# A decoder layer with 32 experts: the expert weights fetched in 2 MB transfers of 16 KB rows, in ten double slots

## What is computed

```python
logits = xt @ w_router + b_router
top_val, top_idx = lax.top_k(logits, 4)
gate = softmax(top_val)
# for each expert e that has rows:
hb = x_pad[rows] @ w_up[e] + b_up[e]                 # w_up[e]  1024 x 2048
glu = minimum(hb[:, :1024], 7); lin = clip(hb[:, 1024:], -7, 7)
act = glu * sigmoid(1.702 * glu) * (lin + 1)
y = act @ w_down[e] + b_down[e]                      # w_down[e] 1024 x 1024
```

## Time and profile before

| | |
|---|---|
| median of 3 runs | 1215.26 us (1214.33 to 1217.21) |
| profiled execution, span | 1214.7 us |
| TensorE busy | 1131.6 us, 93% of the span |
| DMA, q1 (all weight transfers) | 88.9% of 16 engines' span, 441.65 MB |
| HBM read over the span | 364 GB/s |
| SyncE waiting for TensorE in L459 (L1472 and L1508) | 182.4 us |

### The profile page before, as it was taken

How to read it: one execution, slowest core, us unless ns; L and a number is a source line. 1 busy time by engine, 2 the same in 40 slices (tenths; PEclk the granted TensorE clock), 3 DMA queues, 4 the chain that set the end, 5 groups by cost and what they waited for, 6 DMA issues and landing times.

```text
span 1214.7 us, 14754 instructions
## 1 busy us (share of the span) xinstructions
PE 1131.6 (93%) x5609; PEld 506.6 (42%) x5609; DVE 359.5 (30%) x766; ACT 227.4 (19%) x415; POOL 128.5 (11%) x59
## 2 busy tenths in 40 slices
PE   6899999989999999999999979999999899999996
PEld 5788899753333333233333323323222233222222
DVE  4593664632222222122223212222222122222222
ACT  5344554121111111111111111111111111111112
POOL 5562566300000000000000000000000000000000
PEclk9999999989999999999999989999999999999999
DMA  9554235779999999999999999999999999999993
GB/s 355 188 188 147 95 139 190 302 315 359 423 421 421 421 422 419 420 421 421 421 421 421 421 420 421 421 421 421 422 421 421 420 421 422 421 421 421 421 421 145
DMA packets 77890, 444.33 MB, mean 366 GB/s; under 512 B 9166, under 2 KB 12664, under 8 KB 28664
## 3 DMA queue, kind: packets, MB, share of 16 engines
q1 hardware_dynamic: 75904, 441.65, 88.9%
q10 hardware_dynamic: 1912, 1.66, 0.5%
HBM read 441.65 MB, written 1.05 MB: 364 GB/s over the span
## 4 chain that ended last, share of the span: by engine, by line
PE 55%; DMA 19%; SPq 15%; DVE 5%; ACT 3%; issue 3%; POOL 0%; DVEq 0%; ACTq 0%
PE psum L1472 21%; SPq L459 15%; PE psum L1173 11%; PE psum L1508 11%; DMA ring<-in_w_up 9%; DMA gate_area<-in_w_up 5%; DMA qk_area<-in_w_up 4%; PE psum L1427 3%; PE psum L1360 2%; DVE gate_area L1110 1%; DVE gate_area L1106 1%; DVE gate_area L1104 1%; PE psum L1495 1%; ACT gate_area L766 1%; PE psum L1481 1%
## 5 line engine op out<-in xcount | busy, mean ns | idle before, releaser
L1472 PE MATMUL psum<-ring,gate_area 128*64 128x512 f32 x1312 | 311.4, 610 | 28.4 <-DMA ring<-in_w_up 18.4
L1076 DVE TENSOR_TENSOR h_s<-psum,h_s 128x512 f32<-128x512 f32 x132 | 82.0, 683 | 433.2 <-PE psum L1427 433.2
L1472 PEld LDWEIGHTS psum<-ring,gate_area 128*64 128x64 f32 x1312 | 90.2, 139 | 234.5 <-issue 170.6
L1508 PE MATMUL psum<-ring,gate_area 128*64 128x512 f32 x640 | 145.8, 595 | 5.3 <-ACT gate_area L766 5.3
L531 POOL TENSOR_TENSOR unit_lo<-ring,unit_hi 128x1024 fp32r<-128x1024 f32 (+1 forms) x54 | 128.1, 2377 | 95.5 <-ACT unit_hi L564 95.4
L760 ACT ACTIVATE gate_area<-gate_area 128x512 f32<-128x512 f32 x32 | 20.1, 629 | 545.5 <-DVE gate_area L1102 545.5
L1102 DVE TENSOR_SCALAR gate_area<-psum 128x512 f32<-128x512 f32 x32 | 22.1, 692 | 283.5 <-PE psum L1481 283.5
L1508 PEld LDWEIGHTS psum<-ring,gate_area 128*64 128x64 f32 x640 | 44.4, 136 | 86.2 <-issue 76.9
L1427 PE MATMUL psum<-pT_s,gate_area 64*128 64x512 f32 x264 | 65.6, 615 | 0.7 <-ACT pT_s L770 0.7
L564 ACT ACTIVATE unit_hi<-ring 128x1024 fp32r<-128x1024 f32 (+1 forms) x54 | 55.5, 1032 | 47.5 <-PE psum L1173 47.4
L1408 PE MATMUL psum<-xn_area,gate_area 128*64 128x512 f32 x264 | 63.8, 604 | 0.4 <-DVE gate_area L1048 0.4
(11 more groups left out here) (256 smaller groups left out, 1229.1 us busy)
## 6 DMA issues: line engine op xcount, KB each, us to landing
ring<-in_w_up SPq DMA_DIRECT2D x164, 1024.0 KB, 26.5
ring<-in_w_down SPq DMA_DIRECT2D x80, 1024.0 KB, 26.9
gate_area<-in_w_up SPq DMA_DIRECT2D x16, 1024.0 KB, 27.0
xT_area<-in_w_up SPq DMA_DIRECT2D x16, 1024.0 KB, 27.1
ring<-in_w_gate SPq DMA_DIRECT2D x6, 2048.0 KB, 8.7
qk_area<-in_w_up SPq DMA_DIRECT2D x12, 1024.0 KB, 26.5
mem_s<-in_w_up SPq DMA_DIRECT2D x12, 1024.0 KB, 28.2
yl_area<-in_w_up SPq DMA_DIRECT2D x12, 1024.0 KB, 26.9
```

What stands on the lines that cost most here:

```text
L1076: nc.vector.tensor_tensor(h_s[:, b, cols], psum[:, BACK_BANKS[j], :], h_s[:, b, cols], ALU.add).then_inc(added, 1)
L1472: ins = nc.tensor.matmul(psum[lo:lo + SLOTS, c, :], lhsT, w[:, at:at + 512], start=(k == 0), stop=False)
L1508: ins = nc.tensor.matmul(psum[c * SLOTS:(c + 1) * SLOTS, DOWN_BANK, :], lhsT, w[:, at:at + 512], start=(f == 0), stop=(f == KC - 1))
```

## The change

Two neighbouring pieces become one of 2 MB (`PIECE_W` is 4096 numbers, 16 KB, per partition). An expert has 4 up pieces and 2 down pieces. `w_up` is regrouped on the host so that partition p of a piece holds rows p of two chunks side by side, and `w_down` so that a piece is contiguous; every DMA is then one contiguous 2 MB block of 16 KB rows. There are ten slots: six in `ring`, four in areas that are made by putting the former areas side by side: `qe_area` (qk and 8 KB per partition that are new), `gm_area` (end of gate and mem), `xv_area` (xT and vp), `my_area` (memT and yl). `ROUND_SKIPS` leaves slot 5 out of the second round and slot 8 out of the fourth, so that a group of 48 pieces closes. TensorE computes the same chunks in the same order; it signals `piece_used` after every second chunk. GpSimd's descriptor scratch is set to 1 KB; GpSimd issues no DMA in either kernel. `graw` lies in `misc` now.

```diff
-PIECES = UP_CHUNKS + DOWN_SLOTS
-WSLOTS = 19
+PIECE_W = 2 * UP_W
+UP_PIECES = UP_CHUNKS // 2
+DOWN_PIECES = DOWN_SLOTS // 2
+PIECES = UP_PIECES + DOWN_PIECES
+WSLOTS = 10
 GROUP = 8
-SLOT_OF = [n % (WSLOTS - 1) + 1 for n in range(5 * (WSLOTS - 1))]
-for _n in (0, 19, 37, 54, 69, 83):
-    SLOT_OF.insert(_n, 0)
+ROUND_SKIPS = ((), (5,), (), (8,), ())
+SLOT_OF = [s for skips in ROUND_SKIPS for s in range(WSLOTS) if s not in skips]
...
-                if n < UP_CHUNKS:
-                    src_w, dst = w_up[0][bass.ds(e, 1), n * P:(n + 1) * P, :].rearrange("a p n -> (a p) n"), wslot[slot]
+                if n < UP_PIECES:
+                    src_w = w_up[bass.ds(e, 1), n, :, :].rearrange("a p n -> (a p) n")
                 else:
-                    j = n - UP_CHUNKS
-                    src_w = w_down[bass.ds(e, 1), :, j * DOWN_W:(j + 1) * DOWN_W].rearrange("a p n -> (a p) n")
-                    dst = wslot[slot]
-                sp.dma_start(dst, src_w).then_inc(got_piece[slot], 16)
+                    src_w = w_down[bass.ds(e, 1), n - UP_PIECES, :, :].rearrange("a p n -> (a p) n")
+                sp.dma_start(wslot[slot], src_w).then_inc(got_piece[slot], 16)
...
-                            w = piece(u, k, n_group)
+                            w = piece(u, k // 2, n_group)[:, k % 2 * UP_W:(k % 2 + 1) * UP_W]
...
-                            if k < UP_CHUNKS - 1:
+                            if k % 2 == 1 and k < UP_CHUNKS - 1:
                                 ins.then_inc(piece_used, 1)
...
-                            w = piece(u, UP_CHUNKS + j, n_group)
+                            w = piece(u, UP_PIECES + j // 2, n_group)[:, j % 2 * DOWN_W:(j % 2 + 1) * DOWN_W]
...
-                            ins.then_inc(piece_used, 1)
+                            if j % 2 == 1:
+                                ins.then_inc(piece_used, 1)
...
-    nc = bacc.Bacc("TRN2", target_bir_lowering=False, num_devices=1)
+    nc = bacc.Bacc("TRN2", target_bir_lowering=False, num_devices=1, dynamic_dma_scratch_size=1024)
...
+    up = data["w_up"].reshape(NE, UP_PIECES, 2, P, UP_W)
+    data["w_up"] = np.ascontiguousarray(up.transpose(0, 1, 3, 2, 4)).reshape(NE, UP_PIECES, P, PIECE_W)
+    down = data["w_down"].reshape(NE, DOWN_PIECES, 4, P, D)
+    data["w_down"] = np.ascontiguousarray(down.transpose(0, 1, 3, 2, 4)).reshape(NE, DOWN_PIECES, P, PIECE_W)
```

More of the change, by code:

```diff
@@ L187, in hybrid_layer_kernel, with at @@
         xn_parts = nc.alloc_sbuf_tensor_at("xn_parts", [P, 8, S], F32R, offset=xn_at)
-        mem_at = nc.sbuf_base + (-nc.sbuf_base) % 32
-        mem_s = sb("mem_s", [P, B, D])
-        mem_parts = nc.alloc_sbuf_tensor_at("mem_parts", [P, 2, S], F32R, offset=mem_at)
+        def at(name, shape, offset, dt=F32):
+            return nc.alloc_sbuf_tensor_at(name, shape, dt, offset=offset)
+        gm_at = nc.sbuf_base + (-nc.sbuf_base) % 32
+        gm_area = sb("gm_area", [P, 3 * KC * S + B * D])
+        gate_area = at("gate_area", [P, 3 * KC, S], gm_at)
+        mem_at = gm_at + 4 * 3 * KC * S
+        mem_s = at("mem_s", [P, B, D], mem_at)
+        mem_parts = at("mem_parts", [P, 2, S], mem_at, F32R)
+        qe_at = nc.sbuf_base + (-nc.sbuf_base) % 32
+        qe_area = sb("qe_area", [P, PIECE_W])
+        qk_area = at("qk_area", [P, 2 * HEADS // 2 * S], qe_at)
         xT_at = nc.sbuf_base + (-nc.sbuf_base) % 32
-        xT_area = sb("xT_area", [P, KC * S])
-        xT_hi = nc.alloc_sbuf_tensor_at("xT_hi", [P, KC, S], F32R, offset=xT_at)
+        xv_area = sb("xv_area", [P, PIECE_W])
+        xT_area = at("xT_area", [P, KC * S], xT_at)
+        xT_hi = at("xT_hi", [P, KC, S], xT_at, F32R)
+        vp_area = at("vp_area", [P, 2 * HEADS * HD + 2 * B * S], xT_at + 4 * KC * S)
         memT_at = nc.sbuf_base + (-nc.sbuf_base) % 32
[L195 to L202, removed]
+        my_area = sb("my_area", [P, KC * M + 6 * S + 2 * (P + S)])
+        memT = at("memT", [P, KC, M], memT_at)
+        memT_parts = at("memT_parts", [P, 8, S], memT_at, F32R)
+        yT_at = memT_at + 4 * KC * M
+        yl_area = at("yl_area", [P, 6 * S + 2 * (P + S)], yT_at)
+        yT_parts = at("yT_parts", [P, 4, S], yT_at, F32R)
         ib_area = sb("ib_area", [P, S + 2 * (P + S)])
@@ L214, in hybrid_layer_kernel @@
         rope_t = sb("rope_t", [P, 2, 8, ROPE])
-        graw = sb("graw", [64, P])
         gT = sb("gT", [P, 64])
@@ L274, in hybrid_layer_kernel @@
         iw_s = view(misc, 768, B, IHEADS)
+        graw = view(misc, 1024, P)[0:64]
         pooledT = view(pT_s, 0, G, S)
@@ L299, in hybrid_layer_kernel @@
         hot = view(gate_area, 3712, SLOTS // 2).bitcast(BF16)
-        wslot = [ring[:, n * UP_W:(n + 1) * UP_W] for n in range(PIECES)]
-        wslot += [xT_area[:, :], view(mem_s, 0, UP_W), view(gate_area, 4096, UP_W), view(memT, 0, UP_W)]
-        wslot += [view(area, 0, UP_W) for area in (qk_area, vp_area, yl_area)]
+        wslot = [ring[:, n * PIECE_W:(n + 1) * PIECE_W] for n in range(PIECES)]
+        wslot += [view(qe_area, 0, PIECE_W), view(gm_area, 4096, PIECE_W), view(xv_area, 0, PIECE_W),
+                  view(my_area, 0, PIECE_W)]
         y_s = view(pT_s, 0, D // 2)
@@ L451, in load @@
             def load(e, n, slot):
-                if n < UP_CHUNKS:
-                    src_w, dst = w_up[0][bass.ds(e, 1), n * P:(n + 1) * P, :].rearrange("a p n -> (a p) n"), wslot[slot]
-                else:
-                    j = n - UP_CHUNKS
-                    src_w = w_down[bass.ds(e, 1), :, j * DOWN_W:(j + 1) * DOWN_W].rearrange("a p n -> (a p) n")
-                    dst = wslot[slot]
-                sp.dma_start(dst, src_w).then_inc(got_piece[slot], 16)
+                if n < UP_PIECES:
+                    src_w = w_up[bass.ds(e, 1), n, :, :].rearrange("a p n -> (a p) n")
+                else:
+                    src_w = w_down[bass.ds(e, 1), n - UP_PIECES, :, :].rearrange("a p n -> (a p) n")
+                sp.dma_start(wslot[slot], src_w).then_inc(got_piece[slot], 16)
             last = {n % RING_SLOTS: name for n, name in enumerate(FRONT)}
             def load_over(name):
-                for q in range(UP_CHUNKS):
-                    if last[q // 2] == name:
+                for q in range(RING_SLOTS):
+                    if last[q] == name:
                         load(0, q, q)
@@ L476, in _ @@
                       .then_inc(got_parts, 16)
-            sp.wait_ge(bank_filled, FILLED["gate", 3 * KC - 1])
-            load(0, 11, 11)
             sp.wait_ge(bank_filled, FILLED["o", MHEADS + HEADS - 1])
-            load(1, 4, 16)
+            load(1, 0, 6)
             sp.wait_ge(lo_ready, LAST_SPLIT["P"])
@@ L484, in _ @@
             sp.wait_ge(bank_filled, FILLED["br", KC - 1, 2])
-            for q in range(8, 11):
+            for q in range(4, 6):
                 load(0, q, q)
             sp.wait_ge(got_parts, 24 * 16)
-            load(1, 1, 13)
             sp.wait_ge(merged_ready, KC)
-            load(1, 2, 14)
-            load(1, 6, 18)
+            load(1, 1, 7)
             for name in ("O0", "O1"):
@@ L494, in _ @@
                 load_over(name)
-            load(1, 0, 12)
             sp.wait_ge(scaled, 4 * B)
-            load(1, 5, 17)
+            load(1, 2, 8)
             sp.wait_ge(bank_filled, FILLED["logits"])
-            load(1, 3, 15)
+            load(1, 3, 9)
             def load_group(g, first):
@@ L1557 @@
     data["norm_final_g"] = data["norm_final_g"].reshape(1, D)
-    data["w_down"] = np.ascontiguousarray(data["w_down"].reshape(NE, KC, P, D).transpose(0, 2, 1, 3)).reshape(NE, P, KC * D)
+    up = data["w_up"].reshape(NE, UP_PIECES, 2, P, UP_W)
+    data["w_up"] = np.ascontiguousarray(up.transpose(0, 1, 3, 2, 4)).reshape(NE, UP_PIECES, P, PIECE_W)
+    down = data["w_down"].reshape(NE, DOWN_PIECES, 4, P, D)
+    data["w_down"] = np.ascontiguousarray(down.transpose(0, 1, 3, 2, 4)).reshape(NE, DOWN_PIECES, P, PIECE_W)
     for k, v in shape_constants().items():
```

## The result

The changed kernel takes 1203.12 us (median of 4 runs, 1202.4 to 1203.21) against 1215.26 us: 12.1 us less. The ratio is 0.9896, 95% interval 0.9883 to 0.9909. Measured once more later, beside the kernel before, it was 0.991 (0.9882 to 0.9938).

What follows compares the result with a forecast made beforehand. The DMA stream was taken as the bound: span 1214.7 - 10.4 (16 KB rows) + 1.0 (fill and first rounds) + 1.7 (end) = 1207.0, plus 0.6 to the median, said as 1207.5 us. Range 1202 to 1219, the forecast's own 1202 to 1213.

Steps and rivals of the forecast that it cites:

- What bounds: Expert stretch: the DMA stream sets the end, 956 us at 421 GB/s; TensorE is 2.7 us faster per expert.
- 16 KB rows: Weight stream: 1728 fewer packets per engine at 6 ns each, from 2, 4 and 8 KB row times, save 10.4 us.
- The stated upper bound: On the saving from 16 KB rows: 9.3 ns a packet, 16.1 us, using the last five 2 KB slices.
- rival C: Weight stream: a packet costs 9.3 ns, saving 16.1 us, time 1202; part of the forecast's own 0.70.
- Half as many transfers: Full weight stream: a fixed time per transfer lies under the other transfers, so halving their number gives 0.
- The first fill: Before the first release: 20 MB instead of 19, released by two chunks, idle 2.0 instead of 2.4 us: 0.4 better.
- The first rounds: First expert's releases, 280 to 310 us: pauses of 2.5 us, mainly from skipped slot 5, against 1.4 before: 1.1 worse.
- The walk: Release-by-release reckoning of the first rounds' 2 MB transfers, adding pauses of 0.3, 1.8 and 0.4 us to 2.5.
- The end: After the last up piece: two chunks to do instead of one, +1.7 us, no second wait for the down piece.
- The sum: Whole kernel: 1214.7 - 10.4 + 1.0 + 1.7 = 1207.0; with 0.6 to the median 1207.6, said as 1207.5 us.
- A: Weight stream: rate stays at 421 GB/s because rows are cut up or the path is the limit; 1218 us, chance 0.17.
- B: Between last up and first down release: a 7.4 us gap starves the stream; 1219 us with six experts, chance 0.13.

Runs made afterwards that it cites:

- e2: Changed kernel with each partition's 16 KB laid out as four rows of 4 KB, transfers still 2 MB: 1242.4 us, ratio 1.0218 to the kernel before.
- e1: Changed kernel with each partition's 16 KB laid out as two rows of 8 KB, transfers still 2 MB: 1216.61 us, ratio 1.0004 to the kernel before.
- e9: Changed kernel with slot 5 left out of the fifth round instead of the second, measured a second time: 1200.43 us, ratio 0.9882.
- e3: Changed kernel with each 2 MB piece fetched by two transfers of 64 neighbouring partitions: 1991.5 us and three executions of 2085 to 2091.
- e8: Changed kernel with each 2 MB piece fetched by two transfers, one of the even and one of the odd partitions: 1206.89 us, ratio 0.9927.

## Why the prediction was right, and where its size was off

It had the direction and the mechanism; 7.7 us were forecast and 12.1 measured, near the lower end of its own range of 1202 to 1213 us. By its steps:

- **What bounds.** Right. TensorE's busy share, 391 of 400 us, was no sign of a bound: the rate of the stream rose 1.6% and the end came with it.
- **16 KB rows: the step that was mis-sized.** 6 ns a packet were taken, 9.1 measured for a packet of a row: 1536 x 9.1 + 192 x 4.9 = 14.9 us instead of 10.4 (14.5 with 2.5 ns for the closing packets). That is 4.5 us, the size of the miss. It came of the reading for 4 KB rows, "taken as 412" from two stretches of 4 to 5 us each (409 and 416). A sustained stream of such rows runs at 408.3 GB/s (e2). With 409 the prediction's own formula gives 2 x 160.2 - 311.3 = 9.2 ns. The second stretch pulled the figure up by 3 GB/s, less than such short windows scatter, and the difference of two nearly equal times made 2 ns of it. The stated upper bound and rival C, 9.3 ns, came close to the truth, but by luck: they rest on five slices of 2 KB rows and on the same 412.
- **Half as many transfers: 0.** Right, but for their closing packets, which are in the step above (e1 against the kernel before: 294.29 against 294.00 MB in 700 us).
- **The first fill, 0.4 us better.** By the rates of 275 to 285 us, the stream lost 2.87 + 0.27 = 3.1 us before, and 0.74 + 1.81 = 2.5 in e9, whose first steady transfer was issued at 280.14, where the prediction put it: 0.6 better. Right.
- **The first rounds, 1.1 us worse.** The place was right, the skipped slot, the size too small: 285 to 320 us lost 0.4 + 0.1 + 2.0 + 0.9 = 3.4 us in the changed kernel, 0.6 + 0.1 + 0.5 = 1.3 before (the prediction's 1.4 for 280 to 310 us left out the window of 290 to 300): 2.1 us worse. The walk counted pauses; the share reads 0.93 where the rate is 342, so the engines were busier than they were fast just after a pause.
- **The end, 1.7 us.** 1.8 measured, and by the mechanism: from the last up piece to the first down chunk it is 7.67 us (1175.50 to 1183.17), 5.95 before (1190.97 to 1196.92), and TensorE does not wait for the last down piece. Right.
- **The sum.** With the measured terms: -14.9 - 0.6 + 2.1 + 1.8 = -11.6, against -12.1 and -11.4 in the two comparisons of medians, which are certain to 1.6 us in the first and 3.4 in the second. The profiled pair differs by 13.7. Its execution of the kernel before was 1.7 us above the median; and with the early release the stream lost only 0.35 + 0.74 = 1.1 us from 275 to 285 us, not 2.5, which makes the sum for this pair -13.0.
- **The rivals.** A (the rate stays) was refuted by the slices, B (coarse release starves the stream) by full shares from 320 us on, with ten slots and with eight.

The Trainium skill, DMA: Bandwidth & Descriptors, section Rules for kernel authors, gives at least 1 MiB per DMA as the way to the most bandwidth. For the size of a transfer the runs agree (e1: 2 MB transfers gain nothing over 1 MB), but the row length was worth 1.6% in rate beside it, and the rule does not name it. The same page, section Measured, has 425 GB/s for one 16 MB transfer issued from GpSimd; 426.7 were reached here by a stream of 2 MB ones from SyncE.

## What to carry to other kernels

When a stream keeps all DMA engines full, count packets, not transfers: here each row of a transfer was a packet at 9 ns besides its bytes, so doubling the row from 8 to 16 KB gave 1.6% and doubling the transfer at the same row gave nothing. Get such a price from one sustained run at another row length, not from short transfers. And look at the order in which a pool of slots is used in its first rounds: a slot left out early held one transfer back for 3.4 us and cost 2.7 us of the stream, while with the same one left out late the share stays full.

## What was not expected of the hardware

- A stream of transfers that alternate between partitions 0 to 63 and 64 to 127 runs at 217 to 225 GB/s with all engines busy (e3), one that alternates between even and odd partitions at 426.5 (e8).
- The end of a full stream is set by its slowest engines: in the changed kernel the rate falls from 422 GB/s at 1168 to 1172 us to 102 at 1180 to 1184. The 2.7e6 bytes left at 1172 us would take 6.4 us at 427 GB/s and take 12, so some 6 us of the end are theirs, an estimate from these rates.
- The device time was 2.2 to 2.3 us above the profiled span in every execution.
